# Routed experts on one core: passes as further laps of one loop, lists of 128 places, shared down products at the end of the expert block, and sums without GpSimd

## The reference

```python
scores = sigmoid(xf @ router_w)                    # 64 experts
_, idx = top_k(scores + router_bias, 8)            # 8 experts for each of 512 tokens
gates = scores[idx] / sum(scores[idx]) * 2.5
for each expert e:                                 # lists of its tokens
    h = xf[tok]
    y = (silu(h @ w1[e]) * (h @ w3[e])) @ w2[e]    # 1024 -> 256 -> 1024
routed[tok] += y * gate
shared = (silu(xf @ sw1) * (xf @ sw3)) @ sw2       # 1024 -> 256 -> 1024
x = layer_norm(alpha * x + routed + shared)
```

## Time and profile before

| what | value |
|---|---|
| median of three executions | 2248.36 us |
| the profiled execution | 2247.64 us |
| its span, from the first to the last instruction | 2245.9 us |
| mean granted TensorE clock | 0.963 of full |
| TensorE busy | 2092.8 us (93%) |
| VectorE busy | 1649.5 us (73%) |
| ScalarE busy | 1392.2 us (62%) |
| GpSimd busy | 661.3 us (29%) |
| moved by DMA | 595.90 MB, mean 265 GB/s |

### The profile page before, as it was taken

One profiled execution on the slowest core, in us unless ns is written; L12 is line 12 of the kernel. 1 busy time (PEld: TensorE's weight loads), 2 busy tenths in 40 slices (PEclk: granted clock), 3 DMA queues, 4 the chain that ended last, 5 costly groups with the idle time before them and its releaser, 6 DMA issues. The chain is left out here.

```text
span 2245.9 us, 31970 instructions
## 1 busy us (share of the span) xinstructions
PE 2092.8 (93%) x10966; PEld 1630.4 (73%) x10966; DVE 1649.5 (73%) x2297; ACT 1392.2 (62%) x1762; POOL 661.3 (29%) x358
## 2 busy tenths in 40 slices
PE   6999989799999999997779999897999999999957
PEld 4778877677777777775366888775777777777743
DVE  2484453799999999996445834547999999999936
ACT  3542752388888888885034347415888888888831
POOL 0010200044444444443311020002444444444423
PEclk9999999899999999998888999998999999999979
DMA  6312214499999999998931130255999999999977
GB/s 196 94 47 66 95 65 186 155 371 366 376 380 376 372 372 383 380 379 326 373 104 57 59 148 1 83 226 195 376 371 381 382 371 374 377 376 374 370 307 324
DMA packets 135900, 595.90 MB, mean 265 GB/s; under 512 B 29380, under 2 KB 55492, under 8 KB 79736
## 3 DMA queue, kind: packets, MB, share of 16 engines
q1 hardware_dynamic: 102264, 527.43, 62.2%
q0 software_dynamic: 33536, 67.18, 8.9%
HBM read 577.83 MB, written 69.76 MB: 288 GB/s over the span
## 5 line engine op out<-in xcount | busy, mean ns | idle before, releaser
L1383 PE MATMUL ps_up<-w_hi,rowsT_hi 128*112 128x512 f32 x1024 | 424.1, 414 | 14.4 <-DVE rowsT_lo L1477 14.4
L1385 PE MATMUL ps_up<-w_hi,rowsT_lo 128*112 128x512 f32 x1024 | 406.6, 397 | 0.0
L1331 POOL DMA_INDIRECT y_rows<-y,index x128 | 208.8, 1631 | 609.1 <-ACT y L1552 593.3
L1323 POOL DMA_INDIRECT rows<-x_rows,index x128 | 330.6, 2583 | 150.2 <-issue 90.7
L1465 DVE TENSOR_TENSOR w_lo<-w,w_hi 128x2048 fp32r<-128x2048 f32 x128 | 292.6, 2287 | 51.4 <-ACT w_hi L1517 51.4
L1465 DVE TENSOR_TENSOR w_next_lo<-w_next,w_hi 128x2048 fp32r<-128x2048 f32 x128 | 292.7, 2287 | 29.9 <-ACT w_hi L1517 29.9
L1517 ACT CAST w_hi<-w 128x2048 fp32r<-128x2048 f32 x128 | 245.1, 1917 | 49.6 <-PE ps_up L1385 34.0
L1517 ACT CAST w_hi<-w_next 128x2048 fp32r<-128x2048 f32 x128 | 245.1, 1915 | 24.6 <-PE ps_up L1385 24.6
L1383 PEld LDWEIGHTS ps_up<-w_hi,rowsT_hi 128*112 128x112 f32 x1024 | 183.2, 179 | 59.1 <-issue 14.7
L1385 PEld LDWEIGHTS ps_up<-w_hi,rowsT_lo 128*112 128x112 f32 x1024 | 179.9, 176 | 59.9
L1408 PE MATMUL ps_y<-w_hi,hiddenT_hi 128*112 128x512 f32 x512 | 211.1, 412 | 3.9 <-DVE hiddenT_lo L1484 3.9
(11 more groups left out here) (251 smaller groups left out, 4486.6 us busy)
## 6 DMA issues: line engine op xcount, KB each, us to landing
w_next<-exp_w SPq DMA_DIRECT2D x204, 1024.0 KB, 17.6
w<-exp_w SPq DMA_DIRECT2D x136, 1024.0 KB, 8.0
w_first<-exp_w SPq DMA_DIRECT2D x34, 1024.0 KB, 6.6
w_last<-exp_w SPq DMA_DIRECT2D x32, 1024.0 KB
wbuf<-w_in SPq DMA_DIRECT2D x16, 1024.0 KB, 5.6
got<-y_rows SPq DMA_DIRECT2D x8, 2048.0 KB, 24.0
got<-y_rows SPq DMA_DIRECT2D x16, 1024.0 KB, 26.7
w_out_sb<-w_out SPq DMA_DIRECT2D x2, 4096.0 KB, 19.4
```

Of the source, the lines that this page charges most:

```text
L1323: pool.indirect_dma_start(rows[0:CAP, x.slot, :], None, d["x1_rows"], bass.IndirectOffsetOnAxis(ap=index[0:CAP, x.step, 0:1], axis=0), bou ...
L1331: pool.indirect_dma_start(d["y_rows"], bass.IndirectOffsetOnAxis(ap=index[0:CAP, x.step, 1:2], axis=0), y[0:CAP, x.slot % 2, :], None, bou ...
L1383: pe.matmul(ps_up[b][0:CAP], hi, w_hi, start=(k == 0), stop=False)
L1385: mm = pe.matmul(ps_up[b][0:CAP], lo, w_hi, start=False, stop=(k == KD - 1))
```

## The change

1. CAP becomes 128, and the numbers are ordered over the partitions by a new function, `_places`.
2. The loop over passes goes. One `_experts` block runs its laps from a register: laps 1 to `last` - 1 in the hardware loop and then the lap `last`, which is 7 if each expert has at most 128 tokens, and 8 more for each further 128. The expert of a turn is its number modulo 64. `_mix_and_route` computes the further laps instead of the passes. The last lap no longer picks, gathers or compares for turns behind the end.
3. Instead of `next_pass`, each turn lowers one expert's column of places by 128 just behind `hots` (`shifted`), with waits on the turn before.
4. The 11 spare loads and the wait for them go. In their place SP loads the shared down matrix, gain and shift into `rows` once the last rows are turned.
5. `y` becomes two tiles, one of which lies in `w_chunk`. The PSUM tiles of the sums are shared by both blocks.
6. TensorE computes the shared down products of all four token tiles behind the last expert's `down`, in the expert block; the third of them waits until `y` has been read from its tile.
7. In `_second_norm` GpSimd does nothing. TensorE adds place 4 besides places 0 to 3. VectorE adds places 5 to 7 in two instructions and x times alpha in a third, so the scaling at the end of `_mix_and_route` goes.

```diff
-CAP = 112
-SPREAD = 7
+CAP = P
...
+def _places():
+    j, held = np.arange(CAP), np.zeros(CAP)
+    e, r = j % 16, j // 16
+    b6, b4, b3, b2 = e >> 3 & 1, e >> 2 & 1, e >> 1 & 1, e & 1
+    b5, b1, b0 = b2 ^ (r >> 2), b6 ^ (r >> 1 & 1), b4 ^ (r & 1)
+    held[b6 * 64 + b5 * 32 + b4 * 16 + b3 * 8 + b2 * 4 + b1 * 2 + b0] = j
+    return held
...
-                step(dve.tensor_copy(sb["passes"][:], cnt[:, MAX_PASSES - 1:MAX_PASSES]))
+                step(dve.tensor_scalar(cnt[:, 0:1], cnt[:, MAX_PASSES - 1:MAX_PASSES], float(NE // LAP), -float(NE // LAP), ALU.mult, ALU.add))
+                step(dve.tensor_copy(sb["laps_more"][:], cnt[:, 0:1]))
                 gated(1)
                 dve.wait_ge(S["gated"], 2)
-                dve.wait_ge(S["x1_out"], 16 * NT)
-                dve.wait_ge(S["x1T_made"], NT)
                 dve.wait_ge(S["hot_ready"], FIRST + 1)
-                for t in range(NT):
-                    o = dve.tensor_scalar(x_sb[:, t, :], x_sb[:, t, :], ALPHA, None, ALU.mult)
-                o.then_inc(S["scaled"], 1)
-                dve.wait_ge(S["scaled"], 1)
+                step(dve.tensor_scalar(posm[:, :, 0:FIRST + 1], posm[:, :, 0:FIRST + 1], float(CAP), None, ALU.subtract))
...
-        self.expert = self.n % NE if self.known else self.n
+        self.expert = self.n % NE
...
-        return not self.known or 0 <= self.n + k < NE
+        return self.n + k >= 0 if self.known else not self.final or self.step + k < LAP
...
-    with eng.Fori(1, NE // LAP - 1) as lap:
+    with eng.Fori(1, last) as lap:
...
-        step(Turn(NE // LAP - 1, s))
+        step(Turn(last, s, final=True))
...
-                for e in range(SLOTS):
-                    sp.wait_ge(S["up_made"], NE - SLOTS + e + 1)
-                    _load_up(sp, d, sb, l, e, S["ahead_in"])
-                    if e:
-                        sp.wait_ge(S["down_made"], NE - SLOTS + e)
-                        _load_down(sp, d, sb, l, e - 1, S["ahead_in"])
-                sp.wait_ge(S["ahead_in"], EARLY)
+                sp.wait_ge(S["rows_turned"], LAST.n + 1)
+                sp.dma_start(rows[:, 0:2], d["sh_w2"][bass.ds(l, 1)].rearrange("o (m p) c -> p (o m) c", p=P)).then_inc(S["tail_in"], 16)
+                for k, name in ((2, "ln2_g"), (3, "ln2_b")):
+                    sp.dma_start(rows[:, k, :], d[name][bass.ds(l, 1)].to_broadcast([P, D])).then_inc(S["tail_in"], 16)
+                sp.wait_ge(S["tail_in"], 48)
...
-                _laps(pe, step)
+                _laps(pe, last, step)
                 turn_hidden(LAST)
                 down(LAST)
+
+                def shared(t):
+                    for c in range(2):
+                        cols = slice(c * 512, (c + 1) * 512)
+                        for m in range(2):
+                            mm = pe.matmul(sums[t][:, cols], sb["shared"][:, m, t * P:(t + 1) * P], rows[:, m, cols],
+                                           start=(m == 0), stop=False)
+                    return mm
+
+                pe.wait_ge(S["tail_in"], 48)
+                for t in (0, 1, 3):
+                    shared(t)
+                pe.wait_ge(S["y_made"], LAST.n + 1)
+                shared(2).then_inc(S["shared_made"], 1)
...
+                    if x.n_at_least(LAP):
+                        dve.wait_ge(S["shifted"], x.n - FIRST - 3)
                     dve.tensor_tensor(hot[:, b], ...)
+                    if x.n_at_least(FIRST + 2):
+                        column = posm[:, :, bass.ds((x + -1).expert, 1)]
+                        dve.wait_ge(S["hot_ready"], x.n - FIRST - 1)
+                        dve.tensor_scalar(column, column, float(CAP), None, ALU.subtract).then_inc(S["shifted"], 1)
...
-            @block.gpsimd
-            def _(pool):
-                for t in range(NT):
-                    pool.wait_ge(S[f"y{t}a_in"], 16)
-                    pool.tensor_tensor(got[:, t, TOPK - 2, :], got[:, t, TOPK - 2, :], got[:, t, TOPK - 1, :], ALU.add).then_inc(S["paired"], 1)
...
-                    for part, slots in (("b", range(QUARTER)), ("c", range(QUARTER, HALF))):
+                    for part, slots in (("a", (HALF,)), ("b", range(QUARTER)), ("c", range(QUARTER, HALF))):
...
-                    dve.wait_ge(S["joined"], t + 1)
-                    dve.tensor_reduce(half[:, t % 2, :], got[:, t, HALF:TOPK - 1, :].rearrange("p s c -> p c s"), AX.X, ALU.add
-                                      ).then_inc(S["half_summed"], 1)
+                    dve.wait_ge(S[f"y{t}a_in"], 16)
+                    dve.tensor_tensor(out, got[:, t, HALF + 1, :], got[:, t, HALF + 2, :], ALU.add).then_inc(S["half_step"], 1)
+                    dve.wait_ge(S["half_step"], steps + 1)
+                    dve.tensor_tensor(out, out, got[:, t, HALF + 3, :], ALU.add).then_inc(S["half_step"], 1)
+                    dve.wait_ge(S["half_step"], steps + 2)
+                    steps += 2
+                    dve.scalar_tensor_tensor(out=out, in0=x[:, t, :], scalar=ALPHA, in1=out, op0=ALU.mult, op1=ALU.add
+                                             ).then_inc(S["half_summed"], 1)
...
-                    passes = nc.values_load(sb["passes"][0:1, 0:1], min_val=1, max_val=MAX_PASSES)
-                    with nc.Fori(0, passes) as _:
-                        _experts(nc, d, sb, l)
+                    last = nc.snap(more + (NE // LAP - 1))
+                    sb["ps_sum"] = [kept.enter_context(nc.psum_tensor(f"ps_sum{t}", [P, D], F32)) for t in range(NT)]
+                    _experts(nc, d, sb, l, last)
```

More of the change, by code:

```diff
@@ L1253, with _experts @@
 EARLY = (2 * SLOTS + EARLY_DOWN) * 16
-def _experts(nc, d, sb, l):
+def _experts(nc, d, sb, l, last):
     with ExitStack() as ctx:
@@ L1285, in _experts @@
         HALF = KD // 2
+        LAST = Turn(last, LAP - 1)
         with nc.Block() as block:
@@ L1291, in load @@
                 def load(x):
[L1293 removed]
+                    e = bass.ds(l * NE + x.expert, 1)
                     if x.has(-SLOTS):
@@ L1337, in step @@
                         put(x + -2)
-                    gather(x + FIRST)
-                _laps(pool, step)
+                    if x.has(FIRST):
+                        gather(x + FIRST)
+                _laps(pool, last, step)
                 put(LAST + -1)
@@ L1342, in _ @@
                 for s in range(2):
-                    pool.wait_ge(S[f"y{s}_out"], 16 * (NE // 2))
-                for s in range(FIRST):
-                    pool.wait_ge(S[f"rows{s}_in"], 16 * (NE // SLOTS))
+                    pool.wait_ge(S[f"y{s}_out"], 16 * LAST.times(2))
+                    pool.sem_inc(S["dma_turns"], 1)
             @block.tensor
@@ L1415, in step @@
                 def step(x):
-                    pick(x + FIRST)
+                    if x.has(FIRST):
+                        pick(x + FIRST)
                     up(x, 0)
@@ L1491, in step @@
                 def step(x):
-                    if x.known and x.n + FIRST + 1 == NE:
-                        next_pass()
-                    hots(x + (FIRST + 1))
-                    indices(x + FIRST)
+                    if x.has(FIRST + 1):
+                        hots(x + (FIRST + 1))
+                    if x.has(FIRST):
+                        indices(x + FIRST)
                     if x.has(-1):
@@ L1504, in step @@
                     dn_lo(x)
-                _laps(dve, step)
+                _laps(dve, last, step)
                 hidden_lo(LAST)
@@ L1570, in step @@
                         scaled(x + -1)
-                _laps(act, step)
+                _laps(act, last, step)
                 hidden_hi(LAST)
@@ L1589, in _second_norm @@
         st = T("st5", [P, 5, NT])
-        gain, shift = T("gain2", [P, D]), T("shift2", [P, D])
-        ps = [ctx.enter_context(nc.psum_tensor(f"ps_sum{i}", [P, D], F32)) for i in range(NT)]
+        gain, shift = sb["rows"][:, 2, :], sb["rows"][:, 3, :]
+        ps = sb["ps_sum"]
         ident = sb["ident"][:]
@@ L1623, in _ @@
                 halves = [slice(0, 512), slice(512, 1024)]
-                def shared(t):
-                    for cols in halves:
-                        for m in range(2):
-                            pe.matmul(ps[t][:, cols], sb["shared"][:, m, t * P:(t + 1) * P], w2[:, m, cols], start=(m == 0), stop=False)
-                def places(t):
-                    for part, slots in (("b", range(QUARTER)), ("c", range(QUARTER, HALF))):
+                for t in range(NT):
+                    for part, slots in (("a", (HALF,)), ("b", range(QUARTER)), ("c", range(QUARTER, HALF))):
                         pe.wait_ge(S[f"y{t}{part}_in"], 16)
@@ L1636, in places @@
                     mm.then_inc(S["summed"], 1)
-                pe.wait_ge(S["shared_in"], 16)
-                shared(0)
-                shared(1)
-                for t in range(NT):
-                    places(t)
-                    if t + 2 < NT:
-                        shared(t + 2)
             @block.scalar
```

68 lines of the change are left out of this document (29 added, 39 removed).

## The result

The changed kernel takes 2211.81 us (median of four, 2211.63 to 2213.43) against 2247.81 us before on the same chip: ratio 0.9841, 95% interval 0.9826 to 0.9855. The profiled executions have spans of 2245.9 and 2210.1 us.

What follows compares the result with a forecast made beforehand. TensorE's issue was taken to set each expert turn, 9.74 us. Terms 7.7 - 1.4 - 1.0 + 0.1 - 16.8 = -11.4 took 2247.64 to 2236 us; own range 2229 to 2243, 8 in 10 2220 to 2252.

Steps and rivals of the forecast that it cites:

- The turn: Expert block: lists of 128 lengthen each turn by 0.06 us on TensorE, +7.7 us over 128 turns (0 to +17).
- The five short matmuls of `pick`: Uncovered list matmuls in each expert turn, 0.24 us: grow at most with the columns, 16 in 112, so 0.034 us.
- Rival 2: Expert turns: bf16 load takes half at 128 columns, picks save 0.12 us, turn shrinks about 0.1; 2215 us; chance 0.05.
- VectorE and ScalarE in a turn: Expert turn: wider operations and the new column subtraction add 0.42 us, fitting VectorE's reserve of 0.46 plus 0.06; cost zero.
- rival 3: Expert turn: VectorE's chain becomes the bound, TensorE waits for `rows_lo` at each first `up`; +19, 2255 us; chance 0.11.
- The last lap: End of expert block: no picks for three turns, 3 times 0.24 us per layer on TensorE; -1.4 us.
- The block's end: Last `down` to second norm: products of 13.7 us plus 3.1 for barrier and resets replace the spare-load wait; +0.1 us together.
- rival 4: Expert block's end: shared products run at the lower clock, 27.4 us instead of 13.7, twice; up to 2263 us; chance 0.05.
- The second norm: Second norm: fewer loads, earlier last piece and shorter tail, 54.9 us instead of 63.4; -16.8 us (-10 to -20).
- the loads alone: Second norm, lower end of its gain: only the 2.1 MB fewer count, 4.95 us at 424 GB/s; -10 us.
- The end of mixing: End of mixing: of four VectorE scalings only what lies behind the third gather goes, 0.5 us a layer; -1.0 (0 to -4).
- the small additions: End of mixing: two small additions behind the count, placed behind the third gather too; no size of their own.

Runs made afterwards that it cites:

- before_pick128: Kernel before, lists still 112 places but their one-hot columns stored 128 wide (last 16 zero), so only the picks load 128 columns; 2235.65 us, ratio 0.9941.
- before_lists128: Kernel before with only the lists of 128 places, the new order of places and `y` in two tiles; 2238.99 us, ratio 0.9957.
- after_lists112: Changed kernel with `CAP` back at 112 and the old order of places; 2222.76 us, ratio 0.9885.
- after_spare: Changed kernel with the 11 spare loads and their wait put back behind its own three tail loads; 2227.66 us, ratio 0.9903.
- after_late_loads: Changed kernel with all four tiles' shared products at the second norm's start and the shared matrix, gain and shift loaded in that norm again; 2213.18 us, ratio 0.984.
- after_late: Changed kernel with all four tiles' shared products moved to the second norm's start, the three loads staying early; 2203.01 us, ratio 0.9797.
- before_norm: Kernel before with only the new sums, GpSimd's additions and the mixing-end scalings gone; products and loads stay in the second norm; 2242.92 us, ratio 0.9975.
- before_no_spare: Kernel before without the 11 spare loads at the expert block's end and without their wait; 2236.19 us, ratio 0.994.
- after_pick127: Changed kernel with its four list matmuls loading 127 columns, one fewer; the matmul with ones goes first and keeps 128; 2224.66 us, ratio 0.9891.

## Why the prediction was wrong, point by point

**The turn: the step that failed.** "The five short matmuls of `pick` ... grow at most with the columns, 16 in 112, so 0.034." They became shorter by 0.10 (0.24 to 0.14). A turn was forecast 0.06 us longer and is 0.065 shorter, 16 us over 128 turns, two thirds of the 24 that the forecast is off. The rest of that step was a little too dear: for loads behind short instructions and transposes it took 0.03 a turn, and widening them changed the turn by 0.002 (before_pick128 to before_lists128); the covered loads stayed covered. The rule that was weighed there, of the Trainium skill (TensorE: Matmul & The Clock Gate, section on Fast Weight Load), asks for 128 weights and a type that is not FP32; these runs agree for bf16 (131 ns at 112, 143 at 127, 97 at 128). The load did not become twice as fast, as that section has it: 97 ns is two thirds of 143. The fp32r loads, which were the only argument against it, show no discount (176 ns at 112, 189 at 128): a type without the fast load said nothing about one with it. Rival 2 had the right amount for the picks, 0.1 us, and got a chance of 0.05. Its chance was the real mistake, since the only rows against it were of the type that the rule excludes. That the time fell near rival 2's 2215 is in part luck: its turns and last lap would have given 14.4 us and the blocks gave 9.3, while the block's end and the norm gave 8.8 more than it took from the forecast.

**VectorE and ScalarE in a turn** were costed at nothing. That held nearly: VectorE's reserve went from 0.46 to 0.27, though the turn shrank instead of growing, and the column subtraction moves the next start by 0.07 only, so rival 3's 19 us did not come. But the 43 late first `up`s look like a small piece of that rival. The turn of before_pick128 is 0.01 us shorter than the changed kernel's (9.672 and 9.682), so as an estimate they cost some 1.3 us in all. That VectorE causes them is argued and not shown.

**The last lap** was forecast at -1.4. Its last three turns are 0.35 us shorter in layer two, at the full clock in both kernels; in layer one they are 1.95 shorter, of which 1.6 is the clock (last section).

**The block's end.** Products of 13.7 us: 13.9 measured, and at the full clock, so rival 4 fell. The mis-sized term is "the barrier and resets behind it take about 3.1 us". Behind the last product SP needs 0.95 (2.6 and 3.0 in after_lists112, unexplained). The 3.1 were read from the end of DMA traffic to SP's issue, so they are the tail behind a transfer; after_spare shows 3 us once more behind its loads. That is 2.1 us per layer, 4.2 in all. That the vanished spare loads bring next to nothing beside the products was the right reading of two waits of similar length: alone, their removal is worth 12.4 us, and keeping them in the changed kernel costs 15.9.

**The second norm** was forecast at 54.9 us and took 52.6. What was mis-sized is the landing of the last piece: 46.85 us behind SP's first issue by the sum, at most 44.2 in the trace, 2.6 us a layer. The step that failed is the reading of the row it came from, "took 8.83 us instead of 7.03 ... so the last piece landed about 2231.2". TensorE did not wait there. Weight loads of these sums, and windows (last three columns granted clock, DMA share and GB/s), in the kernel before:

```profile
2226.84 0.34 PEld L1635 LDWEIGHTS ps_sum<-got,ident 128*128 128x128 f32 x1 [0.52 <-issue]
2227.69 0.34 PEld L1635 LDWEIGHTS ps_sum<-got,ident 128*128 128x128 f32 x1 [0.52 <-issue]
...
2230.22 0.19 PEld L1635 LDWEIGHTS ps_sum<-got,ident 128*128 128x128 f32 x1 [0.24 <-issue]
2230.65 0.19 PEld L1635 LDWEIGHTS ps_sum<-got,ident 128*128 128x128 f32 x1 [0.24 <-issue]
```

```profile
2226.00:2227.00 1.00, 1.00 (x2) 0.48 (x3) 0.93 (x2) 0.03 (x1) 1.00 (x1) 0.50 1.04 347
2230.00:2231.00 1.00, 1.00 (x3) 0.38 (x2) 1.00 (x2) 0.00 (x0) 0.00 (x0) 1.00 0.07 26
```

The first four sums follow each other at about 0.86 us, at a granted clock of 0.50, the others at 0.43: that is the 1.8 us. 2231.2 was only the latest time at which the piece can have landed, and DMA was nearly idle a microsecond earlier. The first layer's last sums end at 1124.65, which puts its piece at 49.9 us or earlier and, less the 4.95, at 45.0. The tail behind the piece was nearly right, 3.43 + 4.62 against 8.4. In the kernel before 3.5 us more stood in it, from TensorE's end (2234.67) to VectorE's last normalization (2238.19), and that these would go was right. The lower end of the term, "the loads alone" at -10, happens to be the 10.2 us between after_late_loads and after_late, but by another way: there TensorE starts earlier, and no piece is waited for. And what the sum did not see is that the new sums alone, with the products still inside, make TensorE the bound of that norm (before_norm, 5.6 us).

**The end of mixing** and the small additions: -0.9 against -1.0. This agreement shows little. Up to that first cast the kernel before, before_pick128, before_lists128 and before_no_spare all still have the scalings, and the cast starts anywhere between 415.1 and 417.8 us; in the changed kernel it is 415.3.

As a whole, the parts of the change are worth: lists 9.6 us in the kernel before and 11 in the changed one, 7.7 of them by its turns; the new sums 5.6; the removed spare loads 12.4 alone; the early loads 10.2 where products stand in the norm. They do not add up to the whole, since the waits overlap. Products behind the last `down`, together with early loads, are worth nothing against both left in the norm (2211.8 and 2213.2): they lengthen the block's end by what they save in the norm.

## What to carry to other kernels

When a size crosses to a full 128, price each type of operand by its own rows, and where none exist give the rule that names the size a real chance; here one column decided 12.9 us. Before a long row of matmuls is read as a wait, look at the granted clock beside it. Price a wait from the engine or queue that ends it: what follows a transfer and what follows an instruction are different tails (3 and 0.95 us in the changed kernel, though after_lists112 shows up to 3.0 behind an instruction too). Work that is moved out of a bound stage is best split over the idle times on both sides of the boundary, each piece no longer than the wait that hides it.

## What was not expected of the hardware

A bf16 weight load of 127 columns is slower than one of 112 (143 and 131 ns), and one of 128 is faster than both (97).

In the kernel before, the last three turns of the block take 23.65 us in one layer and 22.07 in the other, by the same instructions. In the slower one the granted clock drops behind the wait of 1.97 us ahead of the last `down`; in the other it stays at 1.00 behind a wait of about the same length. The window of the slower layer, granted clock 0.71, is

```profile
1050.00:1054.00 4.00, 3.17 (x9) 2.35 (x10) 0.73 (x2) 0.04 (x1) 0.96 (x1) 0.71 1.02 415
```

and in the changed kernel the clock is 1.00 there in both layers (21.70 and 21.72). after_pick127 shows both cases, 23.27 and 21.67, before_lists128 too, and before_no_spare and before_norm have the slow case in both layers. That is 1.6 us per layer which can fall either way in an execution, and it is part of the 9.3 us of the block. What decides it is not shown.

The last scatter of `y` is issued 4.9 us behind the start of `scaled` where both results share a tile and 2.0 where they have one each, with 112 places and with 128. Its cause was not tried.
